# Forget-gate columns multiplied with the value columns, in token-stationary blocks of 384, 384 and 264 columns

## The reference

```
...
h = rmsnorm(x, norm1_gain[l])
proj = h @ w_in[l]                      # 2048 x 7176
q_a, f_a, i_a, g_a, q_b, k_b, v_b, f_b = split(proj)   # 7 x 1024 and 8 columns
o_a = hgrn2_mixer(q_a, f_a, i_a, g_a, lb_all[l], hgrn_norm_gain[l])
o_b = fox_mixer(q_b, k_b, v_b, f_b, fox_gate_bias[l])  # logf = log_sigmoid(f_b + bias); c = cumsum(logf)
x = x + concatenate([o_a, o_b]) @ w_out[l]              # scores get c[query] - c[key]
...
```

## Time and profile before

| | |
|---|---|
| runs, median | 2844.51 us (2843.17 to 2844.96, 3 runs) |
| the profiled execution | span 2846.5 us, 40996 instructions; no other time of it is shown |
| TensorE matmul, busy | 2803.9 us (99%), 17275 matmuls |
| TensorE weight load | 2398.9 us (84%) |
| VectorE | 1735.5 us (61%) |
| ScalarE | 1315.8 us (46%) |
| DMA | 504.60 MB, mean 177 GB/s |

### The profile page before, as it was taken

How to read it: one execution, slowest core, us unless ns; L and a number is a source line. 1 busy time by engine, 2 the same in 40 slices (tenths; PEclk the granted TensorE clock), 3 DMA queues, 4 the chain that set the end, 5 groups by cost and what they waited for, 6 DMA issues and landing times.

```text
span 2846.5 us, 40996 instructions
## 1 busy us (share of the span) xinstructions
PE 2803.9 (99%) x17275; PEld 2398.9 (84%) x17275; DVE 1735.5 (61%) x2053; ACT 1315.8 (46%) x1672; POOL 43.6 (2%) x71
## 2 busy tenths in 40 slices
PE   8999899999999999999999999999999999999998
PEld 7888788788888888888888888888888888888886
DVE  5688666654445555555555666655666756665665
ACT  6445333544434443444434545644554444443444
POOL 2000000000000000000000100000000000000001
PEclk9999999999999999999999999999999999999999
DMA  7565214555545656655666555555456555555553
GB/s 232 177 193 176 77 47 150 186 182 192 179 135 183 186 192 192 191 193 183 197 190 189 189 180 190 178 169 174 161 180 198 185 195 190 187 198 192 190 181 132
DMA packets 392420, 504.60 MB, mean 177 GB/s; under 512 B 11360, under 2 KB 285293, under 8 KB 391213
## 3 DMA queue, kind: packets, MB, share of 16 engines
q1 hardware_dynamic: 385149, 490.35, 53.5%
q10 hardware_dynamic: 7088, 11.62, 1.3%
HBM read 499.77 MB, written 2.17 MB: 176 GB/s over the span
## 4 chain that ended last, share of the span: by engine, by line
PE 95%; DVE 3%; ACT 1%; issue 1%; DMA 0%; ACTq 0%; SPq 0%; DVEq 0%
PE PS L639 37%; PE PS L644 33%; PE PS L648 17%; PE PS L864 3%; PE PS L676 1%; DVE wlo L1889 1%; PE PS L996 0%; PE PS L1012 0%; PE PS L804 0%; PE PS L784 0%; PE PS L1045 0%; DMA slab<-in_x 0%; ACT whi L1287 0%; PE PS L819 0%; PE PS L1036 0%
## 5 line engine op out<-in xcount | busy, mean ns | idle before, releaser
L1889 DVE TENSOR_TENSOR wlo<-raw,whi 128x1024 fp32r<-128x1024 f32 x922 | 1127.0, 1228 | 791.1 <-ACT whi L1287 787.5
L1287 ACT ACTIVATE whi<-raw 128x1024 fp32r<-128x1024 f32 x922 | 970.3, 1057 | 963.3 <-PE PS L648 497.9
L644 PE MATMUL PS<-XX,whi 128*128 128x512 f32 (+1 forms) x3856 | 1216.8, 397 | 0.0
L648 PEld LDWEIGHTS PS<-XX,wlo 128*128 128x128 f32 (+1 forms) x3856 | 724.5, 188 | 171.3
L648 PE MATMUL PS<-XX,wlo 128*128 128x256 f32 (+1 forms) x3856 | 759.7, 278 | 0.0
L639 PE MATMUL PS<-whi,act 128*128 128x512 f32 x2240 | 602.1, 391 | 0.0
L644 PEld LDWEIGHTS PS<-XX,whi 128*128 128x128 f32 (+1 forms) x3856 | 589.3, 189 | 2.8 <-DVE wlo L1889 0.6
L639 PEld LDWEIGHTS PS<-whi,act 128*128 128x128 f32 x2240 | 418.0, 188 | 85.3
L639 PE MATMUL PS<-wlo,act 128*128 128x512 f32 x1120 | 344.9, 389 | 0.0
L639 PE MATMUL PS<-whi,XX 128*128 128x512 f32 x1024 | 280.8, 396 | 6.5 <-DVE wlo L1889 5.1
L639 PEld LDWEIGHTS PS<-wlo,act 128*128 128x128 f32 x1120 | 210.2, 188 | 44.0
(11 more groups left out here) (363 smaller groups left out, 1355.5 us busy)
## 6 DMA issues: line engine op xcount, KB each, us to landing
raw<-in_ffn_w SPq DMA_DIRECT2D x128, 1024.0 KB, 5.5
raw<-in_w_in SPq DMA_DIRECT2D x103, 1024.0 KB, 5.0
raw<-in_w_ffn_gate SPq DMA_DIRECT2D x44, 1024.0 KB, 4.9
raw<-in_w_ffn_up SPq DMA_DIRECT2D x44, 1024.0 KB, 4.9
raw<-in_w_ffn_down SPq DMA_DIRECT2D x44, 1024.0 KB, 5.1
raw<-in_w_out SPq DMA_DIRECT2D x32, 1024.0 KB, 5.1
raw<-in_xattn_wk SPq DMA_DIRECT2D x16, 1024.0 KB, 5.2
raw<-in_xattn_wv SPq DMA_DIRECT2D x16, 1024.0 KB, 5.0
```

The costliest lines, as they stand in the source:

```text
L644: T.matmul(ps[0:wd, f, :], whi[:, o:o + wd], b.x[:, kk, :], start=first, stop=False, skip_group_check=True)
L648: mm = T.matmul(ps[0:wd, f, 0:SEQ], wlo[:, o:o + wd], b.x[:, kk, 0:SEQ], start=False, stop=last, skip_group_check=True)
L1287: S.activation(k.whi[:, h % 4, 0:b.size], k.raw[:, t % 4, u * b.size:(u + 1) * b.size], ACT.Copy).then_inc(k.w_hi, 1)
L1889: V.tensor_tensor(k.wlo[:, h % 4, 0:b.size], k.raw[:, h // 2 % 4, u * b.size:(u + 1) * b.size], k.whi[:, h % 4, 0:b.size].bitcast(F32), AL ...
```

## The change

The separate 128-column feature block goes, with its transposes. The last 1032 columns of the projection (1024 values, 8 gates) are multiplied in three token-stationary blocks of 384, 384 and 264 columns, which now stand ahead of Qb0, Kb0, Qb1, Kb1. A tile of theirs holds 4 slices of the contraction, as a 512-column one does. In the evacuation of the third, ScalarE also copies the 8 gate columns, scaled, for each 128 tokens. `fox_prep` moves from the preparation to step 14 of the 28 steps of the heads, the cumulative sums and `gates_act` to step 20; the heads are now spread over the 56 halves of the three value blocks and the four query and key blocks. The first product of the seventh head waits for the copy of the sums out of their shared bank. GpSimd clears the heads' buffers ahead of its copies for the cumulative sums; VectorE no longer waits for the store of the sums ahead of the heads. The first scores wait for Kb0, the third pair's for Kb1. The buffer of the gates moves.

```diff
--- before.py
+++ after.py
@@ -32,6 +32,7 @@
 GH = 8
+VCOL = (384, 384, 256 + GH)
 HCH = 64
...
@@ -49,6 +50,7 @@
 HGRN_STEPS = 28
+GATES_AT = 14
 
...
@@ -110,7 +112,7 @@
 
-        return {512: 4, 256: 8, 2 * LORA + SSD_H: 8, P: 16}[self.ncol]
+        return {512: 4, 384: 4, 256 + GH: 4, 256: 8, 2 * LORA + SSD_H: 8}[self.ncol]
 
...
@@ -278,7 +280,7 @@
         self.Qb, self.Kb, self.Vb = v(b + 8192, GH, SEQ), v(b + 10240, GH, SEQ), v(b + 12288, NT, 1024)
-        self.Fb, self.Fbf = v(b + 14336, NT, 8), v(b + 20552, SEQ)
+        self.Fb = v(b + 14336, NT, 8)
         self.Kd, self.Ke, self.Bb = v(b + 14376, GH, SEQ), v(b + 16424, GH, SEQ), v(b + 18472, GH, SEQ)
...
@@ -291,7 +293,7 @@
 
-        self.gates, self.gates_out = v(b + 20808, SEQ)[0:GH, :], self.nc.dram_tensor("gate_sums", (GH, SEQ), F32).ap()
+        self.gates, self.gates_out = v(b + 19752, SEQ)[0:GH, :], self.nc.dram_tensor("gate_sums", (GH, SEQ), F32).ap()
         self.gate_rows = v(b + 14376, GH, 3 * P)
...
@@ -397,7 +399,7 @@
         self.hsp = Stage(sem, "hgrn_split", act=names("xh", 4), dve=names("xl", 4))
-        self.fp = Stage(sem, "fox_prep", pe="t c", dve="e u n", act="f x l c", pool="cu")
+        self.fp = Stage(sem, "fox_prep", pe="c", dve="e u n", act="x l c", pool="cu")
         self.fo = [Stage(sem, f"fox{n}", pe="s t", dve="mx pr", act="ex pT") for n in range(2)]
...
@@ -414,7 +416,7 @@
             if mode == "tok":
-                parts = [(512,)]
+                parts = widths or [(512,)]
             else:
...
@@ -471,15 +473,16 @@
             put("feat", j, w, 1024 + 512 * j, "feat", dst=self.Fa, func=ACT.Sigmoid, rows=True)
-        self.fb_block = put("narrow", 0, w, 7176 - P, "feat", widths=[(P,)], dst=self.Fbf, rows=True)
         for j in range(2):
...
             put("tok", j, w, 3072 + 512 * j, "tok", dst=self.Ga, func=ACT.Silu, row=1)
+        for j in range(3):
+            put("tok", j, w, 6144 + 384 * j, "tok", widths=[(VCOL[j],)], dst=self.Vb, func=ACT.Copy, row=1, at=384 * j,
+                gates=j == 2)
         for j in range(2):
...
             put("feat", j, w, 5120 + 512 * j, "feat", dst=self.Kb, rows=True)
-            put("tok", j, w, 6144 + 512 * j, "tok", dst=self.Vb, func=ACT.Copy, row=1)
         for half in range(2):
...
@@ -527,8 +530,6 @@
             return self.Qh[b.j % 2][:, two, :]
-        if b.kind == "narrow":
-            return b.arg["dst"].unsqueeze(1)
         return b.arg["dst"][:, 4 * b.j + 2 * b.s:4 * b.j + 2 * b.s + 2, :]
...
@@ -636,7 +637,7 @@
                     for tt in range(NT):
-                        mm = T.matmul(ps[:, tt, :], b.x[:, kk, lo + tt * P:lo + (tt + 1) * P], wt,
+                        mm = T.matmul(ps[:, tt, 0:b.ncol], b.x[:, kk, lo + tt * P:lo + (tt + 1) * P], wt,
                                       start=first and m == 0, stop=last and m == 2)
...
@@ -930,14 +931,6 @@
 
-def narrow_pe(k):
-    T, fb = k.nc.tensor, k.fp
-    T.wait_ge(*k.out_of_psum(k.fb_block))
-    for tt in range(NT):
-        mm = T.transpose(k.PS[:, 4, tt * P:(tt + 1) * P], k.Fbf[:, tt * P:(tt + 1) * P], k.ident[:, :])
-    mm.then_inc(fb.pe, 1)
-
-
 def gates_pe(k):
...
@@ -1022,6 +1015,8 @@
         T.wait_ge(*hg.DVE("O", turn - 1))
+    if turn == 3 and not slot:
+        T.wait_ge(*k.fp.ACT("c"))
     for q in range(NT):
...
@@ -1060,6 +1055,8 @@
     def scores(pair):
+        if pair % 2 == 0:
+            k.wait_both(T, k.blocks_of("feat")[-5 if pair == 0 else -1])
         for e in range(2):
...
@@ -1069,9 +1066,8 @@
         T.wait_ge(*k.hg[n].ACT("q", GH // 2 - 1))
-    k.wait_both(T, k.blocks_of("feat")[-1])
     scores(0)
-    T.wait_ge(*k.out_of_psum(k.blocks_of("tok")[11]))
+    T.wait_ge(*k.out_of_psum(k.blocks_of("tok")[12]))
     yield
...
@@ -1255,16 +1251,12 @@
     rows_pe(k, 1, k.stat[:, 4:6])
-    s.to(k.half_at("narrow", 0) + 4)
-    narrow_pe(k)
-    s.to(k.half_at("feat", 7) + 18)
-    gates_pe(k)
     s.to(k.half_at("tok", 9))
...
     T.wait_ge(*k.hz.POOL("z"))
-    T.wait_ge(*k.fp.ACT("c"))
-    s.spread(heads(hgrn_pe, k, GH, 2), HGRN_STEPS, k.half_at("tok", 11) - 2)
-    s.to(k.half_at("tok", 11))
+    s.spread(at_steps(heads(hgrn_pe, k, GH, 2), {GATES_AT + 6: lambda: gates_pe(k)}), HGRN_STEPS,
+             k.half_at("feat", 11) - 2)
+    s.to(k.half_at("feat", 11))
     s.woven(fox_pe(k))
...
@@ -1292,13 +1284,17 @@
             S.wait_ge(k.w_used, b.last + 1)
-            d = b.arg["dst"][:, :, 512 * j:512 * j + 512]
+            heads = b.ncol - (GH if b.arg.get("gates") else 0)
+            at = b.arg.get("at", 512 * j)
+            d = b.arg["dst"][:, :, at:at + heads]
             if b.number == k.blocks_of("tok")[0].number:
...
                 for tt in range(NT):
-                    ins = S.activation(d[:, tt, :], ps[:, tt, :], b.arg["func"], scale=k.stat[:, 4 + tt:5 + tt])
+                    if b.arg.get("gates"):
+                        S.activation(k.Fb[:, tt, :], ps[:, tt, heads:b.ncol], ACT.Copy, scale=k.stat[:, 4 + tt:5 + tt])
+                    ins = S.activation(d[:, tt, :], ps[:, tt, 0:heads], b.arg["func"], scale=k.stat[:, 4 + tt:5 + tt])
             else:
...
@@ -1686,9 +1682,6 @@
     S, fp = k.nc.scalar, k.fp
-    S.wait_ge(*fp.PE("t"))
-    S.activation(k.Fb, k.PS[:, 4, 0:SEQ].rearrange("p (t n) -> p t n", t=NT)[:, :, P - 8:P],
-                 ACT.Copy).then_inc(fp.act, 1)
     S.wait_ge(*fp.DVE("e"))
...
@@ -1853,14 +1846,15 @@
 
-    s.woven(at_steps(hgrn_prep_act(k), {4: lambda: fox_prep_act(k), 6: lambda: gates_act(k)}), 3, k.half_at("tok", 9))
+    s.woven(hgrn_prep_act(k), 3, k.half_at("tok", 9))
     s.to(k.half_at("tok", 9))
...
     S.wait_ge(*k.hz.POOL("z"))
-    s.spread(heads(hgrn_act, k, GH, 2), HGRN_STEPS, k.half_at("tok", 11) - 2)
-    s.to(k.half_at("tok", 11))
+    s.spread(at_steps(heads(hgrn_act, k, GH, 2), {GATES_AT: lambda: fox_prep_act(k), GATES_AT + 6: lambda: gates_act(k)}),
+             HGRN_STEPS, k.half_at("feat", 11) - 2)
+    s.to(k.half_at("feat", 11))
     s.flush()
-    S.wait_ge(k.w_used, k.half_at("tok", 11))
+    S.wait_ge(k.w_used, k.half_at("feat", 11))
     for n in range(4):
...
@@ -2456,8 +2450,7 @@
     V, fp, Fb, nlf, t = k.nc.vector, k.fp, k.Fb, k.nlf, k.fx3
-    V.wait_ge(*k.out_of_psum(k.fb_block))
-    V.wait_ge(*fp.ACT("f"))
+    V.wait_ge(*k.out_of_psum(k.blocks_of("tok")[12]))
     k.dve(V.tensor_tensor(Fb, Fb, k.rep(k.fxb[:, :], NT), ALU.add))
...
@@ -2623,11 +2616,11 @@
 
-    s.woven(at_steps(hgrn_prep_dve(k), {4: lambda: fox_prep_dve(k)}), 3, k.half_at("tok", 9))
+    s.woven(hgrn_prep_dve(k), 3, k.half_at("tok", 9))
     s.to(k.half_at("tok", 9))
-    V.wait_ge(k.gates_stored, 16)
-    s.spread(heads(hgrn_dve, k, GH, 2), HGRN_STEPS, k.half_at("tok", 11) - 2)
-    s.to(k.half_at("tok", 11))
+    s.spread(at_steps(heads(hgrn_dve, k, GH, 2), {GATES_AT: lambda: fox_prep_dve(k)}), HGRN_STEPS,
+             k.half_at("feat", 11) - 2)
+    s.to(k.half_at("feat", 11))
     s.flush()
...
@@ -2723,14 +2716,14 @@
     final_pool(k, 0, k.gain1)
-    G.wait_ge(*k.fp.DVE("n"))
-    G.tensor_copy(k.CU[:, 0:P], k.triu[:, :])
-    G.tensor_copy(k.CU[:, P:SEQ], k.ones[:, :]).then_inc(k.fp.pool, 1)
     G.wait_ge(*k.hp.DVE("q"))
...
     ins.then_inc(k.hz.pool, 1)
+    G.wait_ge(*k.fp.DVE("n"))
+    G.tensor_copy(k.CU[:, 0:P], k.triu[:, :])
+    G.tensor_copy(k.CU[:, P:SEQ], k.ones[:, :]).then_inc(k.fp.pool, 1)
     G.wait_ge(k.w_used, k.half_at("add", 32))
...
```

## The result

The changed kernel takes **2839.54 us** (median of 21 runs, 2837.69 to 2843.61) against 2844.96 us (21 runs, 2842.63 to 2846.38) of the kernel before in the same comparison: ratio 0.9982, 95% interval 0.9976 to 0.9988. That is 5.4 us by the medians and 5.1 us by the ratio, just inside 0.2%.

A forecast was written before the change was run, and what follows sets the result against it. TensorE was taken to bound the kernel (95% of the chain of waits). Terms 5.46 + 0.79 + 0.99 - 0.95 - 0.6 - 0.15 - 0.1 = 5.4 us gained, 2844.5 to 2839.1 us; range 2837.3 to 2841.8.

The forecast's parts named there:

- 1 and 2, block and evacuation: Behind the Fa blocks: dropping the feature block gains 5.46 us, its evacuation leaving the preparation's second step 0.79 us.
- point 2: Preparation's second late start: without the block's evacuation and the transposes it comes earlier, gain 0.79 us, 0.34 us waiting left.
- 3, the store leaves the preparation: Preparation's third late start: ScalarE's gate copy and DMA issue leave, start 0.99 us earlier, about 1.0 us waiting stays.
- 4, the sums among the heads: Step 20 of the heads: the cumulative-sum matmuls return where TensorE has no slack, loss 0.95 us, no wait.
- 5, value columns: Value blocks: 384- and 264-column matmuls in place of 512-column ones lose 0.6 us, bounds 0.3 and 7.4 us.
- The line: Value blocks: matmul spacing drawn through 256 columns (115 ns) and 512 (227.5 ns), giving 171 and 118.5 ns.
- 6, hand-over: Start of the output projection: a key block evacuated last instead of value banks, loss about 0.15 us.
- 7, chains among the heads: Heads: gate chain at step 14 and normalisation in short halves cost nearly nothing, 0.1 us taken; normalisation fits by 0.3 us.
- more slack: Rival, preparation: the two late starts of 0.34 and 1.0 us halve or vanish, gain 6.1 to 6.7 us; chance 0.12.
- Late heads: Rival: the heads' chain is late in short halves or behind the gate chain, 1.5 to 2.3 us lost; chance 0.13.
- A fixed price per matmul: Rival, value blocks: 74 ns fixed per matmul, point 5's upper bound, 2845.9 us in all; chance 0.04.
- Slower: Rival, value blocks: every matmul takes as long as a 512-column one, 21.2 us more, 2860.3 us; chance 0.03.

The follow-up runs named there:

- Experiment 1: The changed kernel with the 128-column feature block and its evacuation put back, without the transposes: stretch from Fa blocks to output projection 255.61 us, median 2846.03 us.
- experiment 2: The kernel before with only the cumulative sums, their copy and DMA issue moved to step 20 of the heads: stretch 254.33 us, ratio 1.0002.
- experiment 3: The changed kernel with value blocks of 512, 256, 264 columns: stretch 251.15 us, median 2842.25; with 448, 448, 136: 254.25 us, median 2844.71.

## Why the prediction was right, and where it was off

The forecast was 2839.1 us, 5.4 us less, with the edge of 0.2% just out of reach; measured are 2839.54 us, and 4.96 us in the stretch. The mechanism held; that the medians agree to 0.5 us is in part luck, since the stretch gave 0.4 to 0.5 us less than forecast and the medians carry the clock's variation. By its points:

- **1 and 2, block and evacuation** (5.46 + 0.79): from the start of the stretch the second late start came after 18.35 us before, 17.55 us now, with two 512-column halves more done. 0.80 for 0.79. The wait left was forecast as 0.34 us, a distance from when the start was due; by that measure it is 0.32 (1761.66 against 1761.34), of which the profile's idle time shows 0.16. Experiment 1 gives 6.20 us for both by undoing them, against 6.25. The transposes of point 2 gave nothing of their own (experiment 2).
- **3, the store leaves the preparation** (0.99): idle 1.09 us stays, 1.0 was expected, and up to the third late start, at 61.54 us of the stretch before and 59.76 now, with two halves (5.45) more done, the gain is 7.23 us against 7.24 by the sum.
- **4, the sums among the heads** (-0.95): they stand behind a block's last matmul (1933.92) at 1934.12, the next product starts at 1934.87, and the one after that is 0.1 us slow: 0.84 + 0.1. Experiment 2 shows 3 and 4 cancel. TensorE's timeline of the changed kernel there:

```profile
1933.80 0.39 PE L649 MATMUL PS<-XX,wlo 128*128 128x256 f32 x2
1934.12 0.60 PE L939 MATMUL PS<-slab 128*8 128x256 f32 x2
1934.56 0.38 PE L940 MATMUL PS<-triu,slab 128*8 128x128 f32 x2
1934.87 0.73 PE L645 MATMUL PS<-XX,whi 128*128 128x512 f32 x2
```

- **5, value columns** (-0.6) is **the term that was mis-sized: 1.15 us**. The changed kernel's timeline in a 384- and in the 264-column block:

```profile
1848.29 0.85 PE L640 MATMUL PS<-whi,XX 128*128 128x384 f32 x4
1848.98 0.51 PE L640 MATMUL PS<-wlo,XX 128*128 128x384 f32 x2
1849.33 0.85 PE L640 MATMUL PS<-whi,XX 128*128 128x384 f32 x4
...
1882.66 0.64 PE L640 MATMUL PS<-whi,XX 128*128 128x264 f32 x4
1883.14 0.41 PE L640 MATMUL PS<-wlo,XX 128*128 128x264 f32 x2
1883.38 0.65 PE L640 MATMUL PS<-whi,XX 128*128 128x264 f32 x4
```

  Six matmuls take 1.04 us and 0.72 us: 173 and 120 ns, not 171 and 118.5. 192 x 0.173 + 96 x 0.120 = 44.7 us, and from the heads' first matmul to the first scores the kernel takes 156.55 us against 154.45: 2.10 more, 0.94 of it the sums and 1.16 the value blocks. The line went wrong in its lower end: the 115 ns at 256 columns are those of a feature block; token-stationary ones of 256 take 120 (experiment 3). With that, about 13 ns beyond 2.4 columns a nanosecond fit 512 (227), 384 (173) and 256 (120), where the line had 3 ns. It is not exact either: at 264 columns it gives 123 ns and 120 were measured, so that it would make the loss 1.6 us.
- **6, hand-over** (-0.15): 1990.52 to 1993.51 is 2.99 us against 2.85: 0.14.
- **7, chains among the heads** (-0.1): no wait in the changed kernel. The margin said to be 0.3 us is 0.37: VectorE's last normalisation ends at 1887.35 (1886.74 + 0.61), the transposes start at 1887.72. VectorE's timeline of the changed kernel:

```profile
1884.95 0.16 DVE L2486 TENSOR_SCALAR slab<-slab 128x2 f32<-128x2 f32 x1
...
1886.74 0.61 DVE L2491 SCALAR_TENSOR_TENSOR slab<-PS,slab 128x128 f32<-128x128 f32 x2
```

Of the rivals: *more slack* did not happen (of the 2.31 us of idle time at the three starts 0.58 + 0.16 + 1.09 = 1.83 us stayed, 1.25 of it at the two that the rival spoke of). *Late heads* did not happen in this kernel, but did in three variants of it, for 0.9 to 1.7 us each. *A fixed price per matmul* of 74 ns is out, and with it the reading of the rule in the Trainium skill, "TensorE: Matmul & The Clock Gate", section "Back-to-back issue gap", under which 96 more matmuls eat the gain: 1.15 us, not about 6. *Slower*: the value blocks' matmuls take 173 and 120 ns, far from the mean of 192 that it wanted; a floor does exist, 112 ns, but it lies under 256 columns: the widths of 448, 448 and 136 give 4.85 us away, most of it there.

## What to carry to other kernels

Where one engine bounds, an operation's worth is its own time on that engine plus what it holds up in the queue that feeds it; find the second in the timeline of the feeding engine, as the time between the operation and the split behind it. Work that sits in the shadow of a late start costs nothing there and its full time elsewhere, and cutting the cause of the late start is worth more than moving what hides in it (1.45 us for two exchanged lines). A late start costs more than the idle time printed for it, here by 0.3 us. When a matmul is made narrower, take the price of the nearest width in the same order of operands, and stay above the width at which the spacing stops falling with the columns (here somewhere between 256 and 136).

## What the runs showed of the hardware that was not expected

- Spacing of token-stationary matmuls, each with its own 128x128 load, at full clock: 227 ns at 512 moving columns, 206 at 448, 173 at 384, 120 at 264 and at 256, 112 at 136. In a feature block the 256-column ones take 115. The 448-column ones are some 6 ns over the others' line; why is open.
- The granted clock differs between executions of the same instructions, in two places (0.97 to 1.00 from 345 to 480 us, 0.79 and 1.00 from 498 to 506 us), and with it the time ahead of the changed stretch, by 3.16 us between the two profiled executions shown.
